# A Strassen exchange on half of the projections' contraction, with the softmax scaling moved to ScalarE

## The reference

```python
z = jnp.einsum('bld,dc->blc', h, w_in)     # fox q,k,v,gate (16 heads of 64), forget logits,
                                           # window q (16 heads), k, v (4 heads), gate
lf = jax.nn.log_sigmoid(ff + b_f)          # fox: causal attention, scores + c_q - c_k, c = cumsum(lf)
p = jax.nn.softmax(...)                    # window heads: 128 back, bias table, sink in the sum
fo, so = fox(...) * silu(fg), swa(...) * silu(sg)
out = jnp.einsum('blc,cd->bld', concat([fo, so]), w_out)
y = layer_norm(ALPHA * h + out, ln_g, ln_b)
```

## Time and profile before

| | |
|---|---|
| median of 3 runs | 1066.47 us (1066.45 to 1066.72) |
| the profiled execution | 1065.04 us, span 1063.5 us |
| busy: TensorE | 1048.2 us (99%), 7,587 matmuls |
| busy: VectorE, ScalarE, POOL | 565.5 (53%), 421.6 (40%), 51.4 us (5%) |
| DMA | 106.64 MB, mean 100 GB/s |

### The profile page before, as it was taken

How to read it: one execution, slowest core, us unless ns; L and a number is a source line. 1 busy time by engine, 2 the same in 40 slices (tenths; PEclk the granted TensorE clock), 3 DMA queues, 4 the chain that set the end, 5 groups by cost and what they waited for, 6 DMA issues and landing times.

```text
span 1063.5 us, 19599 instructions
## 1 busy us (share of the span) xinstructions
PE 1048.2 (99%) x7587; PEld 981.1 (92%) x7587; DVE 565.5 (53%) x1206; ACT 421.6 (40%) x968; POOL 51.4 (5%) x103
## 2 busy tenths in 40 slices
PE   8999999999999999999999999999999999999996
PEld 7999999999999999999999999999999878888884
DVE  6655464544636455364544565544665574332586
ACT  6434343434435344353434454334544552111300
POOL 2010000000000000000000000000000000000000
PEclk9999999999999999999999999999999999999998
DMA  9143123132222223123522212122121154222423
GB/s 337 56 138 108 57 102 112 51 120 93 72 90 102 81 81 120 66 77 112 196 75 93 88 47 79 47 101 94 61 73 61 66 198 140 79 79 100 176 61 118
DMA packets 20808, 106.64 MB, mean 100 GB/s; under 512 B 3216, under 2 KB 3632, under 8 KB 11488
## 3 DMA queue, kind: packets, MB, share of 16 engines
q1 hardware_dynamic: 14960, 83.13, 22.1%
q0 software_dynamic: 5808, 22.95, 6.5%
HBM read 95.18 MB, written 14.17 MB: 103 GB/s over the span
## 4 chain that ended last, share of the span: by engine, by line
PE 97%; DVE 1%; DMA 1%; ACT 0%; SPq 0%; issue 0%; DVEq 0%; ACTq 0%
PE ps L1186 63%; PE ps L1340 19%; PE ps L1310 5%; PE ps L1286 4%; PE ps L1269 2%; PE ps L1270 2%; PE ps L1219 1%; PE ps L1325 1%; DMA x_raw<-in_xT 1%; PE ps L1289 0%; DVE rows L1155 0%; DVE rows L1165 0%; ACT k L685 0%; SPq L498 0%; DVE xl L980 0%
## 5 line engine op out<-in xcount | busy, mean ns | idle before, releaser
L1186 PE MATMUL ps<-xh,wh 128*128 128x288 f32 (+1 forms) x1664 | 504.7, 303 | 0.4 <-DVE wl L988 0.4
L1186 PE MATMUL ps<-xl,wh 128*128 128x288 f32 (+1 forms) x1664 | 492.7, 296 | 0.0
L1186 PE MATMUL ps<-xh,wl 128*128 128x288 f32 (+1 forms) x1664 | 492.4, 296 | 0.0
L1186 PEld LDWEIGHTS ps<-xh,wh 128*128 128x128 f32 x1664 | 313.0, 188 | 6.6 <-issue 4.1
L1186 PEld LDWEIGHTS ps<-xl,wh 128*128 128x128 f32 x1664 | 313.5, 188 | 0.0
L1186 PEld LDWEIGHTS ps<-xh,wl 128*128 128x128 f32 x1664 | 312.8, 188 | 0.0
L825 DVE TENSOR_TENSOR wl<-w_raw,wh 128x1024 fp32r<-128x1024 f32 x132 | 160.2, 1221 | 98.8 <-ACT wh L650 97.7
L1340 PE MATMUL ps<-wh,mix_parts 128*128 128x512 f32 x576 | 185.4, 391 | 0.0
L650 ACT ACTIVATE wh<-w_raw 128x1024 fp32r<-128x1024 f32 x132 | 137.9, 1053 | 77.1 <-PE ps L1340 70.0
L702 ACT ACTIVATE tb<-tb,small 128x256 f32<-128x256 f32 (+5 forms) x160 | 81.3, 509 | 145.8 <-DVE small L915 101.4
L1340 PEld LDWEIGHTS ps<-wh,mix_parts 128*128 128x128 f32 x576 | 108.1, 188 | 23.3 <-issue 1.0
(11 more groups left out here) (126 smaller groups left out, 791.8 us busy)
## 6 DMA issues: line engine op xcount, KB each, us to landing
w_raw<-in_w_all SPq DMA_DIRECT2D x66, 1024.0 KB, 4.8
cbc<-c_rows POOLq DMA_DIRECT2D x16, 360.0 KB, 4.1
x_raw<-in_xT SPq DMA_DIRECT2D x7, 592.0 KB, 10.3
rows<-in_x_p POOLq DMA_DIRECT2D x4, 1024.0 KB, 5.5
out_y_p<-rows SPq DMA_DIRECT2D x16, 256.0 KB, 2.5
rel_copies<-rel_rows POOLq DMA_DIRECT2D x1, 3072.0 KB, 13.6
out_fvT<-vT POOLq DMA_DIRECT2D x8, 296.0 KB, 3.5
out_fkT<-kT POOLq DMA_DIRECT2D x8, 296.0 KB, 2.8
```

The lines of the kernel that those rows point to most:

```text
L1186: ins = nc.tensor.matmul(ps[:, st.bank(k, h), 0:width], a[k % 2][:, w], b[:, ko, first:first + width], start=(ko == 0 and i == 0), stop=(k ...
```

## The change

**Exchange.** Two projection tiles of a pair now form a "duo" (vg, qk or gq). For the first 8 of the 16 chunks, the weights (two groups of 4 chunks, two tiles) and x (two groups of 4 chunks, two halves of the tokens) are 2x2 blocks. Seven block products of weight sums and x sums (x sums `raw7`, `raw6`, `raw3` and x21 - x22 are made once) replace eight; their results are combined in `take_six`, `take_seven`, `take_five` and `join`. The other 8 chunks are multiplied as before (`plain`). A duo takes 15 units of 12 matmuls. The first duo (v and g of pair 0) is multiplied as before. Per duo VectorE makes four weight sums (`make_seven`, `make_five`, `make_six`, `make_four`) and ScalarE and VectorE split five pieces of 512 and three of 1024 columns.

**Scaling.** ScalarE scales the probabilities by their reciprocals (`scale_rows`); VectorE keeps the reciprocal and the 32 meta columns.

**What follows from room in SBUF.** `mixT` holds two pairs; each gated pair is stored to DRAM by POOL (`store_mixed`) and loaded again by SP for the output projection (5 loads, 14 pairs). The weights are loaded in halves (FRONT, BACK) by SP, each when its last reader is done. v and k are written by VectorE's `join`. In the opening, gate computations come after the x sums and the first front part.

The core of the diff:

```diff
...
+CUT = KO // 4
+CUT_LEN = CUT * P
+HALF = TOK // 2
+SUMS_AT, GATES_TURNED_AT, V_FIRST_AT = 2, 5, 11
...
+        if final:
+            score = [2 * i + 1 for i in range(5)]
+        elif len(duos) == 2:
             score = [3 * i + 2 for i in range(5)]
         else:
-            score = [2 * i + 1 for i in range(5)]
-        turn = [x + 4 for x in score]
+            score = [2, 4, 6, 8, 9]
+        turn = [x + 4 for x in score] if final or len(duos) == 2 else [6, 8, 9, 12, 13]
...
-            with engine.Fori(1, FOX_PAIRS) as g:
-                run(Stretch("vgqk", 4 * g, own=Fox, pair=g, kv=g, kind=Fox, g=g - 1, kvs=g))
+            run(Stretch(["qk"], 1, own=Fox, pair=0, kv=0, first=True))
+            run(Stretch(["vg", "qk"], 2, own=Fox, pair=1, kv=1, kind=Fox, g=0, kvs=1))
...
+            def store_mixed(g):
+                pool.wait_ge(gated, 2 * g + 2)
+                pool.sem_inc(pool_passed, 1)
+                src = mixT[:, bass.ds(g & 1, 1), :].rearrange("p a n -> p (a n)")
+                pool.dma_start(mix_rows[bass.ds(g, 1)].rearrange("a p n -> p (a n)"), src).then_inc(mix_stored, 16)
...
+            def four_part(d):
+                act.wait_ge(four_made, d)
+                nc.scalar.activation(wh[1][:, B], w_sum[:, B], ACT.Copy).then_inc(four_high, 1)
+            def keep_first(st, k):
+                act.wait_ge(unit_done, st.after(k, 0))
+                if st.first:
+                    act.wait_ge(silu_done, 2)
+                else:
+                    act.wait_ge(bottom_summed, st.duo(k) - 1)
+                nc.scalar.activation(first_part[:], ps[:, TOP, 0:HALF], ACT.Copy).then_inc(first_kept, 1)
...
+            def scale_rows(st, i):
+                act.wait_ge(recip_done, 5 * st.g + i + 1)
+                first = N_META if st.kind.meta(QTILE[i]) else 0
+                for head in range(2):
+                    row = tb[:, i % SLOTS, head, first:st.kind.keys(QTILE[i])]
+                    nc.scalar.activation(row, row, ACT.Copy, scale=recip[:, i % 3, head:head + 1]).then_inc(scaled, 1)
...
+                seven_part(1, (passed, 2))
+                six_part(1, (passed, 2))
+                for h, done in enumerate((v_read, v_first)):
+                    act.wait_ge(projected[h], 1)
+                    if h == 0:
+                        keep_meta(ps[:, 0, 0:N_META])
+                    nc.scalar.activation(vT[:, h * HALF:(h + 1) * HALF], ps[:, h, 0:HALF], ACT.Copy).then_inc(done, 1)
+                back_parts(1, 0, (projected[1], 1))
...
+                        if u == 10:
+                            evacuate(st, k, 1, 0)
+                        if u == 13:
+                            evacuate(st, k, 0, 1)
+                        if u == 1:
+                            five_part(d, (unit_done, st.after(k, 0)))
+                        if u == 2:
+                            right_part(d, (unit_done, st.after(k, 1)))
+                        if u == FIRST_SUM_AT and st.first:
+                            sum_five()
+                        if u == 4:
+                            four_part(d)
+                            back_parts(d, 1, (projected[1], 2) if st.first else (unit_done, st.after(k, -1)))
+                        if u == 8 and not last:
+                            front_parts(d + 1, (unit_done, st.after(k, 6)))
+                        if u == 11 and not last:
+                            seven_part(d + 1, (unit_done, st.after(k, 10)))
+                            six_part(d + 1, (unit_done, st.after(k, 7)))
...
                     for i in st.at(st.score_at, s - 1):
                         probabilities(st, i)
...
+            def make_five(d):
+                dve.wait_ge(front_loaded[0], 16 * d)
+                dve.wait_ge(seven_made, d)
+                nc.vector.tensor_tensor(w_raw[1][:, A], w_raw[1][:, A], w_raw[0][:, A], ALU.add).then_inc(five_made, 1)
...
+            def make_six(d):
+                dve.wait_ge(five_made, d)
+                dve.wait_ge(front_low, d)
+                nc.vector.tensor_tensor(w_raw[0][:, A], w_raw[0][:, A], w_sum[:, A], ALU.add).then_inc(six_made, 1)
+            def make_four(d, free):
+                dve.wait_ge(six_low, d)
+                dve.wait_ge(*free)
+                nc.vector.tensor_tensor(w_sum[:, B], w_raw[0][:, A], w_raw[0][:, B], ALU.add).then_inc(four_made, 1)
...
+            def take_six(st, k):
+                dve.wait_ge(first_kept, st.duo(k))
+                dve.wait_ge(unit_done, st.after(k, 1))
+                if k:
+                    dve.wait_ge(silu_done, 2 * st.pair + 2)
+                nc.vector.tensor_tensor(diff_part[:], ps[:, SIDE, 0:HALF], first_part[:], ALU.subtract).then_inc(diff_made, 1)
+            def take_seven(st, k):
+                dve.wait_ge(unit_done, st.after(k, 2))
+                dve.wait_ge(diff_made, st.duo(k))
+                nc.vector.tensor_tensor(mid_part[:], ps[:, BOTTOM, 0:HALF], diff_part[:], ALU.add).then_inc(mid_made, 1)
...
+            def take_five(st, k):
+                dve.wait_ge(unit_done, st.after(k, 6))
+                dve.wait_ge(mid_made, st.duo(k))
+                if st.duos[k][0] == "g":
+                    dve.wait_ge(silu_done, 2 * st.pair + 1)
+                five = ps[:, BOTTOM, 0:HALF]
+                nc.vector.tensor_tensor(diff_part[:], five, diff_part[:], ALU.add).then_inc(over_made, 1)
+                nc.vector.tensor_tensor(last_part[:], five, mid_part[:], ALU.add).then_inc(under_made, 1)
...
+            def join(st, k, f, h):
...
+                a, d = result(tile, h), st.duo(k)
+                bank, part_ready, last, op, summed = {
+                    (0, 0): (TOP, first_kept, 5, ALU.add, corner_summed),
+                    (1, 0): (SIDE, over_made, 9, ALU.add, side_summed),
+                    (0, 1): (TOP, mid_made, 12, ALU.subtract, top_summed),
+                    (1, 1): (BOTTOM, under_made, 14, ALU.add, bottom_summed)}[f, h]
+                dve.wait_ge(unit_done, st.after(k, last))
+                dve.wait_ge(part_ready, d)
...
+                nc.vector.tensor_tensor(out, ps[:, bank, a], part[:, a], op).then_inc(summed, 1)
...
                     dve.wait_ge(total_done, n - 5 * FOX_PAIRS)
...
-                first = 0
                 if st.kind.meta(QTILE[i]):
-                    first = N_META
+                    dve.wait_ge(recip_done, n)
                     nc.vector.tensor_tensor(tb_meta[:, i % SLOTS, :].rearrange("p (h n) -> p h n", h=2),
                                             tb[:, i % SLOTS, :, 0:N_META],
-                                            rc.rearrange("p (h o) -> p h o", o=1).broadcast_to([P, 2, N_META]), ALU.mult)
-                for head in range(2):
-                    row = tb[:, i % SLOTS, head, first:st.kind.keys(QTILE[i])]
-                    nc.vector.tensor_scalar(row, row, rc[:, head:head + 1], None, ALU.mult).then_inc(scaled, 1)
...
+                front_parts(1)
+                dve.wait_ge(own_made, 3)
+                gate_logs()
+                make_seven(1, (passed, 2))
+                make_five(1)
+                make_six(1)
+                seven_part(1)
+                six_part(1)
...
                 bias_table()
-                dve.wait_ge(zeros, 7)
...
-                silu(st, 1, 0)
+                back_parts(1, 0)
+                for h in range(2):
...
-                        read_out(st, k - 1, 1)
+                for s in range(st.end + 1):
+                    k, u = divmod(s, UNITS)
...
+                    if u == 0 and 1 <= k <= len(st.duos):
+                        join(st, k - 1, 1, 1)
+                        ready = (k - 1, 1, 1)
+                    if inside:
+                        if u == 2:
+                            take_six(st, k)
+                        if u == 3:
+                            take_seven(st, k)
+                        if u == 6:
+                            join(st, k, 0, 0)
+                            ready = (k, 0, 0)
+                        if u == 7:
+                            take_five(st, k)
+                        if u == 10:
+                            join(st, k, 1, 0)
+                            ready = (k, 1, 0)
...
+                    if ready is not None:
+                        split(st, *ready)
...
-                        weights_low(st.n0 + k + 1, (k + 1) % 2, r // 4)
+                    if inside:
+                        d, last = st.duo(k), st.last and k == len(st.duos) - 1
+                        if u == 1:
+                            five_part(d)
+                        if u == 2:
+                            right_part(d)
+                        if u == FIRST_SUM_AT + 1 and st.first:
+                            sum_five()
+                        if u == 3:
+                            make_four(d, (unit_done, st.after(k, 2)))
+                        if u == 4:
+                            four_part(d)
+                        if u == 5:
```

(87 more changed lines are left out.)

678 lines of the change are left out of this document (450 added, 228 removed).

## The result

The changed kernel takes 1091.3 us (median of 4 runs, 1090.1 to 1092.9) beside 1066.5 us for the kernel before on the same chip: a ratio of 1.0237, 95% interval 1.0218 to 1.0256. It is 2.4% slower. I forecast 1054.3 with a range of 1040 to 1067, and gave the slower side 0.09.

A forecast was written before the change was run, and what follows sets the result against it. TensorE, busy 99% of the span, was taken to bound the kernel. 1065.04 - 35.7 saved + 8.7 opening + 7.2 Fox turns + 7.2 window turns + 0.5 final scores = 1052.9, plus 1.4 to the median: 1054.3 us, range 1040 to 1067.

The forecast's parts named there:

- TensorE's saving, 35.7 us: Projections: 180 matmuls a duo instead of 192 save 1.47 us in 19 duos and 1.31 in 6.
- Engine loads and prices: Fox and window stretches: VectorE 46.3 and 25.6 us, ScalarE 34.5 and 22.6, no engine over 80%; scaling 1.3 us for 2x512.
- First Fox turn, 0.9 us in 8 stretches, 7.2: First tile's transposes in a Fox stretch wait for ScalarE's scaling, behind weight splits: 0.9 us each, 7.2 in all.
- Fourth window turn, 1.2 us in 6 stretches, 7.2: Fourth tile's transposes in window pairs: vector engines need 6.8 us against TensorE's 5.6, so 1.2 us wait each.
- The two-duo window stretch is loose: 0.: Window stretch with two duos: enough slack in its orders, so no TensorE wait counted, 0 us.
- Final scores, 0.5: Final stage: its first scores wait for the gating of the pair before, 0.5 us.
- Opening, 8.7 us: Opening: TensorE waits 4.9 us before unit 0 for v's copy, 3.5 before unit 6, 0.3 before unit 8.
- Weights and partial sums: Hand-overs of weight sums and products to units: tightest orders leave two units, 3.3 us; VectorE up to 2 late, 0 counted.
- Rival 3, the clock: The opening wait lowers TensorE's clock to half, adding 3.3 us, at most 5: 1057 us; chance 0.15.
- Rival 2, the other side: One more hand-over before scaling makes each turn a unit later: 1077; chance 0.1, and 0.1 for half, 1061 to 1065.
- 26.5 us of net gain over 14 stretches: Saving of 35.7 less 9.2 us; from 1.9 us late a stretch on, nothing is gained.
- the 1048 to 1060: Whole kernel: the forecast's own range around 1054.3 us, given chance 0.45.

The follow-up runs named there:

- the last kernel but one: Changed kernel with turned fourth tile's copy and cached keys earlier, scaling back on VectorE, and each stretch's first turned tile copied at its step's start; 1046.3 us.
- the kernel that moved the copy: Changed kernel; in one-duo window stretches ScalarE copies the turned fourth tile first in step 13, ahead of q/gate and weight splits; 1075.2 us.
- The two moves: Changed kernel with the turned fourth tile copied first at step 13 and the cached keys split at step 20; 1057.9 us beside 1065.2 before.

## Why the prediction was wrong, step by step

- **TensorE's saving, 35.7 us.** Right. 60.44 us for a Fox stretch without waits against 60.3, and 32.90 less its two waits of 0.20 and 0.26 against 32.4 for a window stretch. Of the 35.7 us the last kernel but one (1046.3) keeps 20.2.
- **Engine loads and prices.** Right enough. ScalarE's scaling measured 1.32 us for 2x512 (1.3) and 0.90 for 2x256 (0.9); Fox VectorE 44.9 us (46.3), ScalarE 33.5 (34.5).
- **First Fox turn, 0.9 us in 8 stretches, 7.2.** Right in kind and size: 0.87 to 1.03 in seven of them, 6.4; the first waited for nothing.
- **Fourth window turn, 1.2 us in 6 stretches, 7.2.** Right: 1.08 in five, 5.4.
- **"The two-duo window stretch is loose: 0."** Right for the stretch itself, which has no wait between 693 and 758. But in the two window stretches that follow one of two duos the first scores waited 1.49 us and the first turn 0.75, and there I had counted nothing. **Final scores, 0.5:** 0.67.
- **Opening, 8.7 us.** The wait for v was 4.67 (4.9). The second was 0.73, not 3.5. VectorE ended the last x sum at 60.9, not 62.4, and TensorE came to unit 6 at 60.2, not 58.9, since its first 18 matmuls ran at half clock: part of what I had as a wait was paid as clock, about 2.0 us of it by the price above, which I had left to a rival. A wait of 0.79 us at unit 13 I had not. In sum 4.67 + 0.73 + 0.79 + 2.0 = 8.2: that it lies near 8.7 is luck, since two errors cancel.
- **Weights and partial sums: "I find VectorE up to 2 us behind in the heaviest steps and count nothing."** This is the step that failed. The 2 us lateness was found; what it does was not followed to the one place without slack, the last join of a stretch, its key splits and the first scores two steps on. I had walked the steps after the join, and taken it as 0.2 to 0.3 late; behind v's copies, two sets of key copies and the cached keys it was late enough for a wait of 1.47 us. Cost 14.9 us in waits, where the kernel before has 0.8; 15.4 with what followed, by the kernel that moved the cached keys.
- **The fifth turn of the window stretches, not counted.** I walked each chain to the transposes that it feeds, but not the one after, which waits for the bank that the fourth leaves. It is the second part of the same failure. 11.7 us in waits; 16.1 with the clock, by the kernel that moved the copy.
- **Rival 3, the clock.** Right in kind, at 0.50 from 45.6 to 52.4, and too narrow: it fell in three more places, each after a pair of waits of which I had missed one or both. The sentence of the Trainium skill that this rival draws on stands in the section "What's actually happening" of that page (TensorE: Matmul & The Clock Gate).
- **Rival 2, the other side.** It asked for loops above 63 and 35 us, and that is what came (63.48, 35.20). Its mechanism was half right: one hand-over too many, but before scores and a bank's release, not before the scaling, which stayed at my 0.9. At 0.09 for slower it was under-priced: it named 26.5 us of net gain over 14 stretches, 1.9 each, against VectorE 2 us behind "in the heaviest steps".

The two moves are a direct proof of the two missed terms: with both, the kernel takes 1057.9, within the 1048 to 1060 that I gave the forecast as its own range. The 3.6 us above 1054.3 are a balance of small misses on both sides (restarts and clock not counted, some waits counted that did not come), and no run takes them apart.

## What to carry to other kernels

Where one engine is 99% busy and the others half, a change that takes work from it but adds hand-overs is priced by its chains, not by its loads: walk the chain into every wait of the engine that binds (what feeds it, and what frees its bank), at the end of a stage as well as in it, and multiply by the stages. If lateness is found anywhere, follow it until something absorbs it before counting nothing. And when such a kernel comes out slower, look at the order within each step first: three moved pieces of work, and the scaling given back to VectorE, turned 2.4% slower into 1.9% faster, while the scaling moved ahead of two awaited things lost 33 us.

## What the runs showed of the hardware

**The clock can fall after short waits close together.** In the changed kernel TensorE stood 1.08 us up to 650.98 and 1.90 us up to 655.83, and the granted clock was then 0.50 (1.2 GHz) from 656.6 to 660.0. The chain has the two prices side by side, 12 matmuls of a unit before it and 12 in it:

```profile
651.71 1.64 PE ps L1615 x12
...
656.48 2.74 PE ps L1615 x12
```

Five window stretches have this pair of waits. The clock fell after two of the pairs in the changed kernel (at 656 and 790) and after four in the kernel with the cached keys moved. In the two kernels in which only the 1.90 was taken away (fourth tile's copy first, both moves) it fell after none of the five waits of 1.08 that stayed. So a wait can cost far more than its length: 1.9 us less of it in a stretch was worth 3.5 where the clock had fallen with it (36.75 to 33.27), and 1.9 where it had not (35.20 to 33.27). What decides in which stretches it falls, the runs don't tell. It can fall in the opening too: in the profile of the kernel with the scaling alone moved it was 0.50 from 14 to 16 us, behind a wait of 2.4 for x that ended at 13.8, and the span was 1065.1 us. The profile of the kernel before has no such fall, waited 2.0 at that place, and spans 1063.5.

**Without the clock, a wait cost 0.03 to 0.28 us more than its length.** Taking away the 1.90 gave 1.93. Taking away 1.01 and 0.46 before the first scores of a Fox stretch gave 1.86 (63.48 to 61.62), 0.20 more for each. A Fox stretch takes 61.60 us in the kernel with both moves, which has one wait of 0.88 in it, and 60.44 without a wait: 1.16 for 0.88, 0.28 more, though these two kernels differ in the scaling's engine too. Over all waits of the changed kernel it comes to 0.16 each if nothing else is in the remainder of the sum above.
